# One fused transformer kernel: earlier ring loads, a re-ordered mixer end, a latent normalised in two parts, one gate after the softmax

## What is computed

```
x = x + 0.5 * swiglu_ffn(rms_norm(x, ffn1_norm), ffn1_w_in, ffn1_w_out)
h = rms_norm(x, mix_norm)
uv, c_q, c_kv, k_rope, z, xbc, dt_raw, gates = split(h @ w_in)
y_a = gmlp_mixer(uv, ...)             # gelu, norm, 128x128 token mixing
y_b = mla_mixer(c_q, c_kv, k_rope)    # rms_norm(c_q) @ w_uq, rms_norm(c_kv) @ w_ukv, causal softmax attention, 8 heads
y_c = ssd_mixer(z, xbc, dt_raw)       # conv of 4 taps, silu, softplus(dt), chunked scan
g = sigmoid(gates)                    # three gates of 1024
merged = g[0] * (y_a @ w_branch[0]) + g[1] * (y_b @ w_branch[1]) + g[2] * (y_c @ w_branch[2])
x = x + merged @ w_out
x = x + 0.5 * swiglu_ffn(rms_norm(x, ffn2_norm), ffn2_w_in, ffn2_w_out)
```

## Time and profile before

| what | us |
|---|---|
| median of 3 runs (1964.43 to 1967.27) | 1966.35 |
| the profiled execution | 1966.4 |
| its span, first to last instruction | 1964.6 |
| PE busy in the span (97%) | 1913.6 |
| DVE busy (47%) | 932.7 |
| ACT busy (36%) | 709.2 |
| mean granted clock of PE | 0.987 |

### The profile page before, as it was taken

One profiled execution on the slowest core, in us unless ns is written; L12 is line 12 of the kernel. 1 busy time (PEld: TensorE's weight loads), 2 busy tenths in 40 slices (PEclk: granted clock), 3 DMA queues, 4 the chain that ended last, 5 costly groups with the idle time before them and its releaser, 6 DMA issues.

```text
span 1964.6 us, 25874 instructions
## 1 busy us (share of the span) xinstructions
PE 1913.6 (97%) x10898; PEld 1571.9 (80%) x10898; DVE 932.7 (47%) x1166; ACT 709.2 (36%) x813; POOL 77.9 (4%) x145
## 2 busy tenths in 40 slices
PE   9999999999999999999999999999999999999998
PEld 8998585577999899985855678998787975759996
DVE  4545134467554445441335674545667431134453
ACT  5543213143554345432131343554223111124542
POOL 0000000000000000000000002000371100000000
PEclk9999999999999999999899999999998899999999
DMA  6545434343553565454344337636444213326353
GB/s 236 175 139 192 147 124 153 129 137 120 193 172 127 192 215 171 142 193 143 128 145 133 132 108 138 229 117 211 149 135 115 65 65 128 129 86 215 128 182 128
DMA packets 192246, 293.06 MB, mean 149 GB/s; under 512 B 7218, under 2 KB 126804, under 8 KB 192164
## 3 DMA queue, kind: packets, MB, share of 16 engines
q1 hardware_dynamic: 189908, 287.72, 43.3%
q0 software_dynamic: 1936, 4.14, 2.0%
q10 hardware_dynamic: 320, 0.01, 0.0%
HBM read 289.49 MB, written 2.36 MB: 149 GB/s over the span
## 4 chain that ended last, share of the span: by engine, by line
PE 89%; DVE 6%; DMA 2%; ACT 2%; issue 1%; POOL 0%; DVEq 0%; SPq 0%; ACTq 0%; POOLq 0%
PE acc L221 17%; PE acc L223 17%; PE acc L222 17%; PE acc L189 15%; PE acc L253 7%; PE acc L416 2%; PE acc L2389 1%; PE acc L203 1%; PE acc L2697 1%; DMA ring<-in_ffn_w_out 1%; DMA ring<-in_ffn_w_in 1%; DVE w_lo L387 1%; PE acc L2094 1%; PE acc L1168 1%; PE turn L314 1%
## 5 line engine op out<-in xcount | busy, mean ns | idle before, releaser
L387 DVE TENSOR_TENSOR w_lo<-ring,w_hi 128x2048 fp32r<-128x2048 f32 x160 | 362.8, 2290 | 271.4 <-ACT w_hi L383 271.0
L221 PE MATMUL acc<-xT_hi,w_hi 128*128 128x256 f32 x1680 | 477.4, 284 | 6.9 <-DVE w_lo L387 6.9
L222 PE MATMUL acc<-xT_lo,w_hi 128*128 128x256 f32 x1680 | 476.3, 284 | 0.0
L223 PE MATMUL acc<-xT_hi,w_lo 128*128 128x256 f32 x1680 | 476.2, 283 | 0.0
L383 ACT ACTIVATE w_hi<-ring 128x2048 fp32r<-128x2048 f32 x160 | 302.1, 1913 | 217.2 <-DMA ring<-in_ffn_w_out 110.2
L221 PEld LDWEIGHTS acc<-xT_hi,w_hi 128*128 128x128 f32 x1680 | 323.5, 193 | 7.3 <-issue 7.1
L222 PEld LDWEIGHTS acc<-xT_lo,w_hi 128*128 128x128 f32 x1680 | 323.5, 193 | 0.1
L223 PEld LDWEIGHTS acc<-xT_hi,w_lo 128*128 128x128 f32 x1680 | 323.5, 193 | 0.0
L189 PE MATMUL acc<-ring,xT 128*128 128x512 f32 (+2 forms) x736 | 300.4, 567 | 0.8 <-DVE xT L2677 0.8
L189 PEld LDWEIGHTS acc<-ring,xT 128*128 128x128 f32 x736 | 139.1, 190 | 152.3 <-issue 139.7
L221 PE MATMUL acc<-w_hi,hT_hi 128*128 128x512 f32 x440 | 172.9, 393 | 4.4 <-DVE w_lo L387 4.4
(11 more groups left out here) (507 smaller groups left out, 2065.8 us busy)
## 6 DMA issues: line engine op xcount, KB each, us to landing
ring<-in_ffn_w_in SPq DMA_DIRECT2D x88, 1024.0 KB, 5.6
ring<-in_w_in SPq DMA_DIRECT2D x48, 1024.0 KB, 5.0
ring<-in_ffn_w_out SPq DMA_DIRECT2D x44, 1024.0 KB, 4.9
ring<-in_w_branch SPq DMA_DIRECT2D x12, 1024.0 KB, 5.0
ring<-in_w_out SPq DMA_DIRECT2D x12, 1024.0 KB, 5.0
ring<-in_w_gate SPq DMA_DIRECT2D x11, 1024.0 KB, 5.2
ring<-in_w_up SPq DMA_DIRECT2D x11, 1024.0 KB, 6.6
ring<-in_w_down SPq DMA_DIRECT2D x11, 1024.0 KB, 5.0
```

The source lines that it names most:

```text
L221: pe.matmul(o, a_hi, wh, start=start, stop=False)
L222: pe.matmul(o, a_hi, wl, start=False, stop=False)
L223: return pe.matmul(o, a_lo, wh, start=False, stop=stop)
L387: vec.tensor_tensor(w_part(w_lo, r), raw_part(c0, r), w_part(w_hi, r).bitcast(F32), ALU.subtract).then_inc(f.lo, 1)
```

## The change

- **Ring loads.** The load of an FFN down chunk no longer waits for PE's products, only for DVE's subtraction (`chunk` in `ffn_sync`). The first four loads of what follows an FFN (the mixer, the next layer's first FFN, the second block) wait for the subtraction too (`raw_freed`).
- **Tail parts.** `part_hi` has four places. The rest is written back into the ring slot (`ring_lo`, the same memory as `ring`); `part_lo` is gone, and ACT's wait for the products of the chunk two before with it.
- **Tail order.** Gate 5's sigmoid and the rounding of branch 1's input stand behind the 16 exponentials on ACT. On PE the softmax transposes come between branch 0 and branch 1, the attention output between branch 1's two chunks; the last branch and the output projection run m by m, and `merged_pe` is cut in two. The fillers in the tail (2, 6, 5 and 6) are removed.
- **Latent.** `cqn` is normalised before the sums of c_kv. The 5 fillers ahead of xbc0 are removed. The dt product is cut in two and put between the tiles of xbc1; the gMLP transposes and `gm_vec3` come later.
- **Norms.** Fillers stand between the transposes of tile 0 and tile 1 (6 or 7; in the mixer's norm 3, where there were none). `apart` holds for the very first norm alone, and the transposes of tile 0 at the end of the second FFN are no longer inside it. In the first norm the gain's transpose and copy come first, and ACT runs one root of a constant before.
- **Second block.** The second groups of the two output projections run m by m (`tile_pe`); one filler more in the cross-attention.

In the diff, cut to its core, what is left out is counting and signatures:

```diff
--- before.py
+++ after.py
...
+        ring_lo = nc.alloc_sbuf_tensor_at("ring_lo", [P, RING, SLOT], F32R, offset=nc.sbuf_base - 4 * RING * SLOT)
...
         def part_act(act, s, c, e, hi, k=4, n=512):
 
             wait_chunk(act, c)
-            if e >= 2:
-                wait_products(act, c - 2)
-            act.activation(hi[:, e % 2], slot(c, k, n), ACT.Copy).then_inc(s.hi, 1)
-
-        def part_vec(vec, s, c, e, hi, lo, k=4, n=512):
+            act.activation(hi[:, e % RING], slot(c, k, n), ACT.Copy).then_inc(s.hi, 1)
+
+        def part_vec(vec, s, c, e, hi, k=4, n=512):
+
             vec.wait_ge(s.hi, e + 1)
-            vec.tensor_tensor(lo[:, e % 2], slot(c, k, n), hi[:, e % 2].bitcast(F32), ALU.subtract).then_inc(s.lo, 1)
+            vec.tensor_tensor(slot_lo(c, k, n), slot(c, k, n), hi[:, e % RING].bitcast(F32), ALU.subtract).then_inc(s.lo, 1)
...
+            if not s.apart:
+                for b in range(4):
+                    turned(b)
...
+        def norm_pe(pe, s, nb=xn, tiles=(0, 1), busy=(0, 0)):
             for b in range(2 * tiles[0], 2 * tiles[-1] + 2):
                 m, hf = b // 2, b % 2
+                if hf == 0:
+                    keep_busy(pe, turn[b], busy[m])
                 pe.wait_ge(s.vec, s.tile(m))
...
+        def raw_freed(f, j):
+
+            return f.lo, RING + N_IN + KF // 2 - RING + j + 1
+
...
             def chunk(r, src, i=0):
-                sync.wait_ge(products_done, c0 + r + 1)
+                if after and r < RING and type(i) is int:
+                    sync.wait_ge(*raw_freed(after, r))
+                elif r < N_IN:
+                    sync.wait_ge(products_done, c0 + r + 1)
                 sync.wait_ge(f.lo, r + 1 + RING * i)
                 sync.dma_start(raw_part(c0, r), src).then_inc(landed[(c0 + r) % RING], 16)
...
-        norms_in = [Norm(norms, (20 * l, 32 * l, 12 * l), l < DEPTH, apart=l > 0) for l in range(DEPTH + 1)]
-
-        def layer_program(l):
+        norms_in = [Norm(norms, (20 * l, 32 * l, 12 * l), l < DEPTH, apart=l == 0) for l in range(DEPTH + 1)]
...
+                for i, (G, c, w) in enumerate(LATENT):
                     wait_products(act, c + 1)
                     for m in range(MT):
                         act.activation(junk[:, 0:w], acc[bank(G, m)][:, 0:w], ACT.Square,
                                        accum_out=stat[:, 16 + 2 * i + m:17 + 2 * i + m]).then_inc(cq.act, 1)
-                        act.wait_ge(cq.act, 2 * i + m + 1)
-                act.activation(stat[:, 20:22], stat[:, 16:18], ACT.Sqrt, bias=eps_col[:, 0:1], scale=1.0 / QR).then_inc(cq.act, 1)
-                act.activation(stat[:, 22:24], stat[:, 18:20], ACT.Sqrt, bias=eps_col[:, 0:1], scale=1.0 / KVR).then_inc(cq.act, 1)
+                        act.wait_ge(cq.act, 3 * i + m + 1)
+                    act.activation(stat[:, 20 + 2 * i:22 + 2 * i], stat[:, 16 + 2 * i:18 + 2 * i], ACT.Sqrt,
+                                   bias=eps_col[:, 0:1], scale=1.0 / w).then_inc(cq.act, 1)
...
+                    vec.wait_ge(cq.act, 3 * i + 3)
+                    vec.reciprocal(stat[:, 24 + 2 * i:26 + 2 * i], stat[:, 20 + 2 * i:22 + 2 * i]).then_inc(cq.vec, 1)
+                    vec.wait_ge(cq.vec, i + 1)
+                    for m in range(MT):
+                        ins = vec.tensor_scalar((cqn, ckvn)[i][:, m, :], acc[bank(G, m)][:, 0:w],
+                                                stat[:, 24 + 2 * i + m:25 + 2 * i + m], None, ALU.mult)
...
-                pe.wait_ge(qs.vec, 50)
-                keep_busy(pe, turn[2], 2)
                 pe.wait_ge(qs.vec, 52)
...
+            def last_branch_pe(pe):
+
+                b = BRANCHES[2]
+                pe.wait_ge(tail.vec, 4)
+                for m in range(MT):
+                    for n in range(2):
+                        ins = split_chunk_pe(pe, tail, G_BR + 4 + n, m, C_BR + 4 + n, 6 + n, yT_hi[:, b], yT_lo[:, b], part_hi)
+                        ins.then_inc(tail.pe if m == 0 else products_done, 1)
+                        if m == 1 and n == 0:
+                            merged_pe(pe, 0)
...
                     if m == 1:
-                        norm_pe(pe, mix_norm, tiles=(1,))
+                        norm_pe(pe, mix_norm, tiles=(1,), busy=(0, 3))
                     pe.wait_ge(mix_norm.vec, mix_norm.turned(2 * m + 1))
                     tile_pe(pe, G_U, C_U, xT, m)
                 group_pe(pe, G_V, C_V, xT, (4, 4), 512)
                 group_pe(pe, G_CQ, C_CQ, xT, (4, 4), QR)
                 gm_mix_pe(pe)
                 group_pe(pe, G_KV, C_KV, xT, (4, 4), KVR + ROPE)
-                keep_busy(pe, turn[2], 5)
                 turned_group_pe(pe, G_XBC0, C_XBC0, xT, 4, 512)
                 cq_pe(pe)
+                turned_group_pe(pe, G_XBC1, C_XBC1, xT, 4, 520, between=dt_pe)
                 gm_turn_pe(pe)
-                dt_pe(pe)
-                turned_group_pe(pe, G_XBC1, C_XBC1, xT, 4, 520)
                 group_pe(pe, G_Z, C_Z, xT, (4, 4), 512)
                 sd_cs_pe(pe)
                 qs_groups_pe(pe)
...
+                branch_pe(pe, 0, 0)
+                branch_pe(pe, 0, 1)
                 qs_pt_pe(pe)
+                branch_pe(pe, 1, 0)
                 qs_pv_pe(pe)
-                branch_pe(pe, 2)
-                merged_pe(pe)
-                wait_acc_free(pe, G_WO, 0)
-                keep_busy(pe, acc[bank(G_WO, 0)], 6)
-                pe.wait_ge(tail.vec, 8)
+                branch_pe(pe, 1, 1)
+                last_branch_pe(pe)
                 for n in range(2):
-                    split_group_pe(pe, tail, G_WO + n, C_WO + 2 * n, 8 + 2 * n, xT_hi, xT_rest, part_hi, part_lo, 2,
-                                   for_x=(n == 1))
+                    for m in range(MT):
+                        pe.wait_ge(tail.vec, 6 + 2 * m)
+                        for i in range(2):
+                            if n == 0 and m == 0 and i == 1:
+                                merged_pe(pe, 1)
+                            ins = split_chunk_pe(pe, tail, G_WO + n, m, C_WO + 2 * n + i, 8 + 2 * n + i, xT_hi[:, 4 * i:4 * i + 4],
+                                                 xT_rest[:, 4 * i:4 * i + 4], part_hi, i == 0, i == 1)
+                            if m == 1:
+                                ins.then_inc(products_done, 1)
+                        if n == 1 and m == 0:
+                            ins.then_inc(tile0_done, 1)
...
                 branch_in_act(act, 0)
+                tail_part_act(act, 2, 3)
+                qs_act3(act, 0)
+                qs_act3(act, 1)
+                gate_act(act, 5)
                branch_in_act(act, 1)
-                tail_part_act(act, 2, 3)
-                gate_act(act, 5)
...
-                gm_vec3(vec)
                 xbc_vec(vec, 0)
                 dt_vec(vec)
+                gm_vec3(vec)
...
                 branch_in_vec(vec, 0)
-                tail_part_vec(vec, 2)
+                tail_part_vec(vec, 2, 3)
+                qs_vec5(vec, 0)
                branch_in_vec(vec, 1)
...
-                    norm_vec(vec, n1, gain0[:, 0:8], between=first_gain_vec)
+                    first_gain_vec(vec)
+                    add_norm_vec(vec, lambda e, m: None, n1, gain0[:, 0:8])
...
-                norm_pe(pe, n1, tiles=(1,) if l > 0 else (0, 1), busy=7 if l > 0 else 18)
                 if l == 0:
                     first_gain_pe(pe)
+                norm_pe(pe, n1, busy=(0, 7) if l > 0 else (18, 0))
                 ffn_pe(pe, f1, n1, C_FFN1, G_FFN1, lambda e: norm_pe(e, mix_norm, tiles=(0,)), asides={7: params_pe})
                 mixer_pe(pe)
-                norm_pe(pe, n2, busy=5)
-                ffn_pe(pe, f2, n2, C_FFN2, G_FFN2, lambda e: norm_pe(e, n_next, tiles=(0,)), asides={4: params2_pe, 6: s5_c_pe} if l == DEPTH - 1 else {})
+                norm_pe(pe, n2, busy=(0, 6))
+                ffn_pe(pe, f2, n2, C_FFN2, G_FFN2, lambda e: None, asides={4: params2_pe, 6: s5_c_pe} if l == DEPTH - 1 else {})
...
+            tile_pe(pe, G_WO2 + 1, C_WO2 + 2, xT, 0, tile0_done)
+            tile_pe(pe, G_WO2 + 1, C_WO2 + 2, xT, 1)
+            norm_pe(pe, nx, busy=(0, 6))
```

293 lines of the change are left out of this document (149 added, 144 removed).

## The result

The changed kernel takes 1942.11 us (median of 4 runs, 1939.69 to 1943.54) against 1965.39 of before in the same comparison (1962.49 to 1967.27). The ratio is 0.9882, with a 95% interval of 0.9864 to 0.9899: 1.2% faster, 23 us. Run again beside other runs of before, it gave 0.9884 (0.9868 to 0.9900). The forecast was 1942.5. Note that this pair differs by some 3 us more than the medians do (23.3).

The account below looks back on a forecast made before the run. PE, busy 97% of the span, was taken to bound the kernel through its own work, waits, fillers and granted clock. The terms summed to -23.9 us, from 1966.4 to 1942.5, with a range of 1929 to 1954.

Parts of the forecast that it names:

- the S5 part: Gated delta and S5 stage: 0 in the sum; rival that its half-clock time shifts, 6 us either way, chance 0.04.
- The tail: Mixer's last part: four PE spaces go, new softmax waits of 5.0 per layer, -12.2; clock fall there, +4.0.
- The latent stage: Gap ahead of xbc0 closes, -5.2; wait ahead of gMLP transposes goes, -2.0; clock fall in dt stage goes, -6.4.
- The 6.4: dt product and xbc1: no more clock fall, gaining about 1.6 in layer 0 and 4.8 in layer 1.
- the clock falls all the same: Rival in the latent stage: the clock still falls, the 6.4 us are not gained, 1949 us; chance 0.13.
- The FFN ends: Five PE waits for `w_lo`, one per FFN, go as down-chunk loads wait for DVE's subtraction: -4.4.
- Where nothing changes: Layer 1's second FFN: the largest single wait, 6.9 us, stands in a place the edit does not touch.
- The mixer's norm: Three fillers ahead of tile 1's transposes delay the norm's end by 1.3 per layer: +2.6.
- The first norm: Very first norm: gain's transpose and copy wait for its load ahead of the fillers, +1.1, between 0.5 and 1.4.
- The second block's output projections: Second groups run m by m: 0, since their residual adds already lie under PE.
- The slower side: Rival: half clock from the softmax wait to the tail's end in each layer, 2038 us; chance 0.04.

Follow-up runs that it names:

- the repeated profile: The changed kernel itself profiled once more, with no edit: 1938.32 us, ratio to before 0.9884.
- both joined kernels: Changed kernel with tile 1's scaling and copies earlier, fewer start fillers, early root on ACT: 1921.85 us; second also without mixer-norm fillers, gain's transpose behind 11 fillers: 1918.93 us.

## Why the prediction was right

The mechanisms held nearly throughout. That the time was met to 0.4 us is partly luck: in the profiles the start was off by +2.05 us and the S5 part by -2.1, which cancel, and seven other terms by 0.3 to 0.9 each, all but one toward a larger gain. The profiled pair came out 2.8 us beyond the forecast's -23.9, and the medians 0.6 short of it. Point by point:

**The tail** (-12.2 and +4.0 of clock, -8.2; measured -8.75) was right as a mechanism and nearly in size. The forecast waits of 1.5 and 3.2 were 1.37 and 3.00, the one at the merged sum 0.46 for 0.25, and the clock's fall cost 1.9 and 1.4, where 2.0 had been taken. The walk along ACT and DVE with the durations of before is what gave this; a sum of the removed spaces alone would have said 22. The parts of the new tail were tested in one place only, gate 5 behind the exponentials; what the four places of `part_hi`, the m by m order and the earlier first loads are worth each, no run shows.

**The latent stage** (-5.2, -2.0, -6.4) was right: -5.5 for the first and -9.3 for the other two together. Undoing the part on `cqn` alone costs 2.5 per layer. The 6.4 was worked out with 5.5, 3.5 and 16.9, where the rows say 5.64, 3.64 and 17.05; by the rows it is 1.7 and 5.0, and what was gained beside the two waits of 1.0 is 7.3. The fall of the clock is gone in both layers. The forecast named two causes of it without choosing. The runs show that the 8-column products in one piece are enough, with no idle time; whether the wait of 1.0 would be enough with those products cut in two, no run tested. The rival "the clock falls all the same" is shown wrong by the granted clock of 1.00.

**The FFN ends** (-4.4) were right as a mechanism and too small in size: all five waits are gone, and undoing the edit cost 6.7. "Where nothing changes", of the largest wait, was not quite so: it came out as 5.5 in two pieces for 6.9 in one.

**The mixer's norm** (+2.6) was right to 0.1; without the fillers the stretch is back at the 8.85 of before.

**The first norm** (+1.1; measured +3.15, and 2.2 in the repeated profile) was mis-sized. The step that failed is "fillers and transposes start up to 1.7 us later": the gain's load let PE go only at 4.70, against 2.19, 2.5 later (4.55 in the repeated profile, and 4.7 is in the waits above). And the forecast missed what `apart` does there: DVE multiplies tile 0 before it scales tile 1, and so waits behind the fillers.

```profile
6.16 0.75 DVE L300 TENSOR_SCALAR xn<-x,stat 128x1024 f32<-128x1024 f32 x1
16.19 1.29 DVE L292 TENSOR_TENSOR xT<-turn,gain 128x512 f32<-128x512 f32 x2 [9.28 <-PE turn L320]
17.39 0.15 DVE L298 RECIPROCAL stat<-stat 128x1 f32<-128x1 f32 x1
17.58 0.75 DVE L300 TENSOR_SCALAR xn<-x,stat 128x1024 f32<-128x1024 f32 x1
```

Tile 1's scaling, possible from 7.3 on, when its root is there, comes at 17.58, and PE waits 1.81 for it.

**The second block's output projections** ("0, their residual adds lie under PE already"): this was wrong for one of the two, by 0.8 us, ahead of the last norm. Timeline of DVE there, after:

```profile
1734.92 0.16 DVE L298 RECIPROCAL stat<-stat 128x1 f32<-128x1 f32 x1 [2.88 <-ACT stat L268]
1735.12 0.75 DVE L300 TENSOR_SCALAR xn<-x,stat 128x1024 f32<-128x1024 f32 x1
1735.79 1.28 DVE L549 SCALAR_TENSOR_TENSOR x<-acc,x 128x512 f32<-128x512 f32 x2
```

Tile 0's root needs a table load of 1.28 on ACT first (from 1733.30 on, right behind tile 0's sum); DVE waits for it, and tile 1's residual add, whose products ended at 1734.98, stands behind tile 0's scaling. With the table loaded earlier (both joined kernels) the 0.8 is gone, to 92.13; in the ten kernels without that line the stretch is 92.6 to 93.1.

**The S5 part** (0; measured -2.1) had been a rival of 6 us either way, at a chance of 0.04 and with no effect on the range. By the experiments that chance was too small: the stage moved by up to 7 us in kernels that don't touch it. That it came out at -2.1 was luck, and what moves it stays open.

**The slower side** did not come: the clock was back at full at about 447.5, some 4 us after the wait's end and within the wide products that follow.

## What to carry to other kernels

When work is moved earlier on the engine that sets the time, walk the feeding engines' rows in order with the durations of the old trace. Here it gave the two new waits to 0.2 us, and the idle time that shows up in such a walk on a feeding engine is where its next operation belongs: two calls moved on DVE gave 12.3 us in the tails, where the whole reordering before had given 8.75. If a row of many narrow matmuls is followed by a fall of the clock, try it cut in two with wide ones between, even if nothing waits there. And stages are to be compared by length between the same two products, since the whole time moves by more than the edit.

## What was not expected of the hardware

- 32 matmuls of 8 columns in a row, between wide ones and with PE never idle, brought the granted clock to half and cost 3.35 us; two pieces of 16 kept it at full.
- An idle time of 2.34 us between wide products left the clock at full; one of 1.37 and one of 3.00 with eight transposes between brought it down, and with fillers in those two it stayed at full.
- One unedited stage (the second block up to the end of the S5 part) took 123.4 to 132.0 us over twelve kernels, with more or less time at half clock, and 125.01 and 125.09 in two profiles of one kernel. Executions of that one kernel took 1937.1 to 1943.5 us, at mean granted clocks of 0.987 to 0.990.
- A table load on ACT stood between two activations with pauses of 0.02 and 0.01 us: it cost its 1.28 us and no more.
